# Recurrence levels as two masked 64-row blocks instead of four 32-row tiles, with single-buffered keys and another order of work

## The reference

```python
def wkv7_scan(r, decay, k, v, a, b, s0, reverse, return_y):
    '''S_t = S_{t-1} (diag(w_t) + a_t b_t^T) + v_t k_t^T ;  y_t = S_t r_t.  S: (B, H, N_value, N_key).'''
    xs = tuple(jnp.moveaxis(t, 1, 0) for t in (r, decay, k, v, a, b))

    def step(s, inp):
        rt, wt, kt, vt, at, bt = inp
        sa = jnp.einsum('bhvk,bhk->bhv', s, at)
        s = s * wt[:, :, None, :] + sa[..., None] * bt[:, :, None, :] + vt[..., None] * kt[:, :, None, :]
        y = jnp.einsum('bhvk,bhk->bhv', s, rt) if return_y else None
        return s, y
    ...
...
    for d, reverse in enumerate((False, True)):
        dc, kc, ac, bc = dirs_c[d]
        s_c, yc = wkv7_scan(r_c, dc, kc, vr_c, ac, bc, s0, reverse, with_ctx_out)
        dl, kl, al, bl = dirs_l[d]
        _, yl = wkv7_scan(r_l, dl, kl, vr_l, al, bl, s_c, reverse, True)
```

## Time and profile before

| | |
|---|---|
| median of 3 runs | 3984.77 us (3971.74 to 3986.89) |
| the profiled execution | 3977.56 us, its span 3975.8 us |
| PE busy | 3472.4 us, 87% of the span |
| PEld busy | 2580.4 us, 65% |
| DVE busy | 1563.2 us, 39% |
| ACT busy | 1099.8 us, 28% |
| POOL busy | 181.2 us, 5% |
| mean granted clock of TensorE | 0.928 of 2.4 GHz |
| opening of the recurrence | 395 to 423 us |
| the six steps | 423 to 852 us |

### The profile page before, as it was taken

How to read it: one execution, slowest core, us unless ns; L and a number is a source line. 1 busy time by engine, 2 the same in 40 slices (tenths; PEclk the granted TensorE clock), 3 DMA queues, 4 the chain that set the end, 5 groups by cost and what they waited for, 6 DMA issues and landing times. The chain is left out here.

```text
span 3975.8 us, 53364 instructions
## 1 busy us (share of the span) xinstructions
PE 3472.4 (87%) x23450; PEld 2580.4 (65%) x23450; DVE 1563.2 (39%) x2379; ACT 1099.8 (28%) x1728; POOL 181.2 (5%) x183
## 2 busy tenths in 40 slices
PE   6989778857888884999997799999999997799999
PEld 5854667744533332888785467887888785467877
DVE  3454655535211114333424544334333424543333
ACT  3235423211000002222323552223222323452222
POOL 0020221201000001000000000000000000000000
PEclk8989778868899996999998899999999999899999
DMA  6130000022599994222211022223222211022220
GB/s 226 64 124 0 3 3 3 3 84 85 212 419 421 421 421 155 85 90 101 85 43 69 1 75 85 95 96 97 93 85 103 88 43 69 1 74 85 85 106 38
DMA packets 173827, 441.02 MB, mean 111 GB/s; under 512 B 5794, under 2 KB 97692, under 8 KB 149020
## 3 DMA queue, kind: packets, MB, share of 16 engines
q1 hardware_dynamic: 173596, 437.61, 29.5%
HBM read 435.49 MB, written 2.10 MB: 110 GB/s over the span
## 5 line engine op out<-in xcount | busy, mean ns | idle before, releaser
L331 PE MATMUL banks<-mix_r,ring_r 128*128 128x512 f32 x1776 | 702.4, 396 | 0.0
L331 PE MATMUL banks<-mix_r,ffn_r 128*128 128x512 f32 x1664 | 666.6, 401 | 14.9 <-ACT mix_r L2324 7.8
L331 PE MATMUL banks<-h_r,ffn_r 128*128 128x512 f32 x1664 | 652.5, 392 | 0.0
L293 DVE TENSOR_TENSOR ring_r<-ring,ffn_r 128x2048 fp32r<-128x2048 f32 (+1 forms) x169 | 359.6, 2128 | 229.3 <-ACT ffn_r L290 226.5
L290 ACT ACTIVATE ffn_r<-ring 128x2048 fp32r<-128x2048 f32 (+1 forms) x169 | 301.3, 1783 | 479.1 <-PE banks L331 472.7
L331 PEld LDWEIGHTS banks<-mix_r,ring_r 128*128 128x128 f32 x1776 | 336.3, 189 | 83.6
L331 PEld LDWEIGHTS banks<-mix_r,ffn_r 128*128 128x128 f32 x1664 | 315.8, 190 | 84.2 <-issue 17.0
L331 PEld LDWEIGHTS banks<-h_r,ffn_r 128*128 128x128 f32 x1664 | 315.6, 190 | 73.6
L2501 PE MATMUL banks<-ring_r,ffn_r 128*128 128x512 f32 x704 | 279.2, 397 | 0.0
L2052 PE MATMUL banks<-ring,arena 128*64 128x512 f32 x1056 | 242.3, 613 | 37.1 <-DMA ring<-in_exp_w_down 23.3
L2500 PE MATMUL banks<-ffn_r 128*128 128x512 f32 x640 | 251.6, 393 | 4.7 <-DVE arena L2453 4.7
(11 more groups left out here) (419 smaller groups left out, 5220.6 us busy)
## 6 DMA issues: line engine op xcount, KB each, us to landing
ring<-in_exp_w_down SPq DMA_DIRECT2D x30, 2048.0 KB, 18.7
ring<-in_w_ffn_gate SPq DMA_DIRECT2D x44, 1024.0 KB, 5.3
ring<-in_w_ffn_up SPq DMA_DIRECT2D x44, 1024.0 KB, 7.9
ring<-in_w_ffn_down SPq DMA_DIRECT2D x20, 2048.0 KB, 7.7
ring<-in_exp_w_gate SPq DMA_DIRECT2D x18, 2048.0 KB, 17.6
ring<-in_exp_w_up SPq DMA_DIRECT2D x18, 2048.0 KB, 17.2
ring<-in_w_in SPq DMA_DIRECT2D x17, 2048.0 KB, 8.1
arena<-in_exp_w_gate SPq DMA_DIRECT2D x14, 2048.0 KB, 18.3
```

Source lines behind the costliest of these rows:

```text
L293: l.did(V.tensor_tensor(lo, x_, hi, ALU.subtract).then_inc(l.sem, 1), name, "lo", v)
L331: ins = TE.matmul(m[1](bank), m[2], m[3], start=m[4], stop=m[5])
```

## The change

The four 32x32 diagonal blocks of A become two 64x64 ones (`Am64`), whose masks (`levm`, now 64 columns) leave only the entries of a level; these lie within the 32x32 diagonal blocks, so X stays packed in 32 columns. A product of a level is then 16 matmuls for each direction, with 64 rows and 64 weight columns and 32 columns moved. The weights of `level_x`, `P1D`, are written by ACT twice from the same PSUM, once times a column of ones in the even 32-row blocks and zeros in the odd, once the other way round (`even`, `odd`, new columns of `hsel`), which puts a block in its place of the diagonal. `begin` makes X's start from the two halves of the masked product. `Al` has room for two levels instead of four, so POOL waits for `P1_made` of two levels before.

The keys have one buffer (`BK(d, e)`). `turn(0)` moves up between levels 2 and 3, `turn(1)` behind `whole_x`; `in_pe` for the next step comes after level 4 and after `turn(1)`, `cum_pe` after `pair_x` and after W. The grams run one to two places earlier, and `gram(1)` uses banks 2 and 3, own products banks 2, 3, 6, 7, U banks 6, 7 and Y banks 0, 1. In the opening both directions' `in_pe` and `cum_pe` come first, direction 1 in banks 0 and 1. The lists of ACT and DVE follow.

```diff
-    lev = np.zeros((2, P, 5, 32), np.float32)
-    c = s % 32
-    k = np.arange(32)[None, :]
+    lev = np.zeros((2, P, 5, 64), np.float32)
+    c = s % 64
...
-    hsel = np.kron(np.eye(2), np.ones((64, 1))).astype(np.float32)
+    hsel = np.concatenate([np.kron(np.eye(2), np.ones((64, 1))), (t[:, None] // 32) % 2 == np.arange(2)[None, :]], -1).astype(np.float32)
...
-                Am32, P1s, X64a = (hole.take(512) for _ in range(3))
-                sum_ = region(hole.at - 3 * 512, 2, 4, P)
-                spare1, spare2, spare3 = (hole.take(4, P) for _ in range(3))
+                sum_ = region(hole.at, 2, 4, P)
+                Am64, P1D = hole.take(16, 64), hole.take(16, 64)
+                P1s = P1D.rearrange("p g n -> p (g n)")[:, 0:512]
+                X64a = hole.take(512)
...
-                BK_even = high.take(2, 2, 4, P)
+                BK_ = high.take(2, 2, 4, P)
...
-                Al = high.take(4, 16, 32)
+                Al = high.take(2, 16, 64)
...
+                in_bank = lambda n, d: 0 if n == 0 and d == 1 else 2
+                even, odd = hsel[:, 2:3], hsel[:, 3:4]
...
                     l.wait_ge(*smalls["rwkv"])
                     in_pe(l, 0, 0)
+                    in_pe(l, 0, 1)
...
+                    cum_pe(l, 0, 0)
+                    cum_pe(l, 0, 1)
...
+                    w_dve(l, 0, 1)
...
-                        if j == 0:
-                            plus_dve(l, 0, 0)
-                    for t in range(NTA):
+                    plus_dve(l, 0, 0)
+                    plus_dve(l, 0, 1)
+                    for t in range(3):
                         vtm_copy(t)
                     kd_dve(l, 0, 0)
-                    l.wait_ge(*past(ro, "bonus_made"))
-                    l.did(V.tensor_copy(bonus.rearrange("p t c -> p (t c)"), banks[:, 4, 0:32]).then_inc(l.sem, 1), ro, "bonus")
+                    kd_dve(l, 0, 1)
+                    for t in range(3, NTA):
...
-                gram_bank = lambda q: 6 if q == 0 else 0
+                gram_bank = lambda q: 2 if q == 1 else 0
+                own_bank = lambda d: 6 if d else 2
...
                             elif q == 1:
                                 l.wait_ge(*past(co, "Amf", 0, 1))
-                            else:
+                            elif q == 2:
+                                l.wait_ge(*past(co, "Gm", 0, 1))
+                            elif q:
...
                             for g in range(8 * d, 8 * d + 8):
-                                for b in range(4):
-                                    ins = TE.matmul(cols_of(lower(d), g)[quad(b)], Al[quad(b), i - 1, g, :], XTp[quad(b), g, :],
-                                                    start=True, stop=True, tile_position=(32 * b, 32 * b))
+                                for hs in halves64:
+                                    ins = TE.matmul(cols_of(lower(d), g)[hs], Al[hs, i % 2, g, :], XTp[hs, g, :],
+                                                    start=True, stop=True, tile_position=(hs.start, hs.start))
...
                             l.wait_ge(*past(co, "P1", i, d))
                             if i == 1:
-                                l.wait_ge(*past(co, "Gm", 0, 1))
+                                l.wait_ge(*past(co, "Amf", 1, 1))
                             for g in range(8 * d, 8 * d + 8):
-                                for b in range(4):
-                                    ins = TE.matmul(cols_of(upper(d), g)[quad(b)], packed(P1s, d)[quad(b), g % 8, :], Xp[quad(b), g, :],
-                                                    start=True, stop=True, tile_position=(32 * b, 32 * b))
+                                for hs in halves64:
+                                    ins = TE.matmul(cols_of(upper(d), g)[hs], P1D[hs, g, :], Xp[hs, g, :],
+                                                    start=True, stop=True, tile_position=(hs.start, hs.start))
...
+                        gram(2)
+                        level_p(2, 0)
+                        level_p(2, 1)
+                        level_x(2, 0)
+                        level_x(2, 1)
+                        gram(3)
+                        turn(0)
+                        level_p(3, 0)
+                        level_p(3, 1)
+                        level_x(3, 0)
+                        level_x(3, 1)
+                        gram(4)
+                        level_p(4, 0)
+                        level_p(4, 1)
+                        level_x(4, 0)
+                        level_x(4, 1)
                         if more:
-                            l.wait_ge(*past(co, "Amf", 1, 1))
+                            l.wait_ge(*past(co, "BKt", 0))
                             in_pe(l, n + 1, 0)
-                        for i in (2, 3, 4):
-                            level_p(i, 0)
-                            level_p(i, 1)
-                            level_x(i, 0)
-                            level_x(i, 1)
-                            if i < 4:
-                                gram(i)
+                        gram(5)
+                        pair_p(0)
+                        pair_p(1)
+                        gram(6)
+                        pair_x(0)
+                        pair_x(1)
                         if more:
                             cum_pe(l, n + 1, 0)
-                        pair_p(0)
-                        pair_p(1)
-                        gram(4)
-                        pair_x(0)
-                        pair_x(1)
-                        gram(5)
                         whole_p()
+                        gram(7)
+                        whole_x()
+                        turn(1)
                         if more:
                             l.wait_ge(*past(nx, "Em", 0))
                             in_pe(l, n + 1, 1)
...
+                            cum_pe(l, n + 1, 1)
                         for d in range(2):
-                            l.wait_ge(*past(co, "XTf", d))
+                            l.wait_ge(*past(co, "XTf", 0))
+                            l.wait_ge(*past(co, "XTf", 1))
...
-                            for b in (0, 1):
-                                l.did(S.activation(packed(Am32, d)[quad(b)].rearrange("p (h j) n -> p h j n", h=2),
-                                                   banks[quad(b), 2 * d:2 * d + 2, :].rearrange("p h (j n) -> p h j n", j=4)[:, :, :, quad(b)],
-                                                   ACT.Copy).then_inc(l.sem, 1), co, "Am32", d)
+                            l.did(S.activation(Am64[0:64, 8 * d:8 * d + 8, :].rearrange("p (h j) n -> p h j n", h=2), own64(d, halves64[0]),
+                                               ACT.Copy).then_inc(l.sem, 1), co, "Am64", d)
...
-                            l.did(S.activation(packed(P1s, d), of32(lower(d)), ACT.Copy).then_inc(l.sem, 1), co, "P1", i, d)
+                            if i < 5:
+                                for x, part in enumerate((even, odd)):
+                                    l.did(S.activation(P1D[:, 8 * d:8 * d + 8, 32 * x:32 * x + 32], of32(lower(d)), ACT.Copy, scale=part)
+                                          .then_inc(l.sem, 1), co, "P1", i, d)
+                            else:
+                                l.did(S.activation(packed(P1s, d), of32(lower(d)), ACT.Copy).then_inc(l.sem, 1), co, "P1", i, d)
...
+                        keys(0)
+                        p1(4, 0)
+                        p1(4, 1)
...
+                        if more:
+                            exps_act(l, n + 1, 1)
...
-                            l.did(V.tensor_tensor(packed_x(d), packed(Am32, d), lm(d, 0), ALU.mult).then_inc(l.sem, 1))
+                            l.did(V.tensor_tensor(P1D[:, gs, :], Am64[:, gs, :], lm(d, 0), ALU.mult).then_inc(l.sem, 1))
+                            l.wait_ge(*l.own())
+                            l.did(V.tensor_tensor(packed_x(d), P1D[:, gs, 0:32], P1D[:, gs, 32:64], ALU.add).then_inc(l.sem, 1), co, "halves", d)
...
                         gm(0, 1)
+                        gm(1, 0)
                         add(1, 0)
+                        gm(1, 1)
                         add(1, 1)
                         gm(2, 0)
                         gm(2, 1)
+                        add(2, 0)
+                        add(2, 1)
                         gm(3, 0)
                         gm(3, 1)
+                        add(3, 0)
+                        add(3, 1)
+                        gm(4, 0)
+                        gm(4, 1)
                         add(4, 0)
                         add(4, 1)
                         if more:
+                            w_dve(l, n + 1, 0)
                         gm(5, 0)
                         gm(5, 1)
                         if more:
+                            kd_dve(l, n + 1, 0)
                         gm(6, 0)
                         gm(6, 1)
                         if more:
+                            plus_dve(l, n + 1, 0)
+                        pairs(0)
```

(53 more changed lines are left out.)

166 lines of the change are left out of this document (68 added, 98 removed).

## The result

The changed kernel takes 3993.2 us (median of 10 runs, 3988.3 to 4000.1), the kernel before 3977.3 beside it (10 runs, 3967.3 to 3990.2): a ratio of 1.0042, with a 95% interval of 1.0030 to 1.0054. So it is slower by some 16 us, 0.4%, where 3942 was forecast; the range, 3912 to 3975, misses it. The profiled execution took 3991.1 us (span 3989.3, before 3975.8).

A forecast was written before the change was run, and what follows sets the result against it. PE's level stage was taken as paced by instruction delivery, one 256-instruction block in 3.75 us. Savings of 5 x 6.2 + 8.0 + 0 = 39 us gave 3938.6 from the profiled 3977.6; with the runs' median, 3942, range 3912 to 3975.

The forecast's parts named there:

- The bound of the kernel before: Level stage: PE stops every 256 instructions, waiting for a block each 3.75 us; 51.0 us of idle time in the recurrence.
- The level products: PE's new 64-row units in the level stage: 0.96 us pitch against about 0.6, using the upper bound of 1.15 us.
- (c): Rival, slower: loads at 1.2 GHz make units 1.8 us through the level stage; 7.4 slower a step, 4022 us; chance 0.09.
- lower bound of 0.45: Level products: half the instructions in half the time, 0.45 us for one direction's 32 matmuls and loads.
- The chain of the level stage: Step 2 from level_p(1,0) at 562.7 to pair_p at 589.0: 26.3 us, pair_p 6.4 us earlier than before.
- I count one low bout as before: +2.3: Level stage: PE's clock is at 1.2 GHz for one 5 us bout, then returns; adds 2.3 us a step.
- The head: DVE's start of each step, ahead of the level products: 0.45 us more for each direction.
- doubling: Bound for the head: new add and larger multiply on DVE take twice as long beside POOL, 1.1 x 2 us.
- The tail: From pair_p to U, with work moved in and out: 0.2 us more a step, the last one 3.0 less.
- opening: Reordered work before the recurrence: pack at 425.6 instead of 426.0, taken as 0, bounds -2 and +3 us.
- (a): Rival, more: the level stage's low-clock bout vanishes because PE no longer stops; saves 53 us, 3925; chance 0.20.
- (b): Rival, nothing: each instruction block in the level stage still brings its stop; 0.6 us a step slower, 3981; chance 0.14.

The follow-up runs named there:

- e2: The changed kernel with each level product again as four 32-row tiles of 32 weight columns; 3997.3 us, ratio 1.0047 to the kernel before.
- e9: e6 with the four 32-row tiles of e2 in each level product; 3992.4 us, ratio 1.0050 to the kernel before.
- e5: The kernel before with 3 and 1 unused dense 128x512 products ahead of level_p(1,0) and level_p(1,1); 3974.5 us, ratio 1.0009.
- e10: The kernel before with 4 and 3 unused dense 128x512 products ahead of level_p(1,0) and level_p(1,1); 3987.9 us, ratio 1.0038.
- e6: The changed kernel with POOL's level-2 Al delayed and 4 and 3 unused dense products ahead of level_p(1,0) and level_p(1,1); 3935.8 us, ratio 0.9908.
- e4: The changed kernel with 3 and 1 unused dense 128x512 products ahead of level_p(1,0) and level_p(1,1); 3966.2 us, ratio 0.9971 to the kernel before.
- e8: The changed kernel with one unused dense product ahead of each of levels 2, 3 and 4, none in the head; 3985.5 us, ratio 1.0031.
- e3: The changed kernel with POOL's Al of level 2 waiting for the second transpose of level 0; 3981.7 us, ratio 1.0010 to the kernel before.
- e1: The kernel before with only the changed kernel's new opening; 3975.1 us, ratio 0.9991.

## Why the prediction was wrong, step by step

**The bound of the kernel before was read rightly.** The stops were the delivery of instructions: they vanish with half the instructions (after), return with twice as many (e2, e9), and hardly care for the clock (e5, e10). In the recurrence of before no two packets of the instruction queue are less than 3.3 us apart. The instruction queue of the changed kernel has 5 packets in 555 to 590 us, where the earlier trace rows have 8 in 30.

**The level products: right.** A unit has a pitch of 1.03 us (forecast 0.96) at 2.4 GHz and 1.8 at 1.2, as the upper bound and rival (c) said. The lower bound of 0.45 is out. The columns moved don't set the time: whole_p, with twice as many behind loads of the same form, had 1.15 for its 32 at 2.4 GHz, `level_p` has 1.12. The load's columns fit; its rows doubled as well, and no run separates the two.

**The chain of the level stage: right at the clock it assumed.** e6 has 26.3 us, the number of the forecast. They agree a bit by luck: the forecast's 26.3 holds 2.3 for a low bout, e6's 2.8 for three dense products. e4's step 0 is the cleaner measure of the chain: 24.6 at 1.00, against 24.0 without the bout, and level_p(1,1) 3.2 us behind level_p(1,0) as the forecast's 3.3 asked.

**The step that failed: "I count one low bout as before: +2.3".** That is some 5 us at 1.2 GHz a stage, 30 in all. From the clocks of the six stages after (0.75, 0.70, 0.66, 0.70, 0.51, 0.52) the low time is 2 x (1 - clock) of each, 162 us of 219.7. In it a unit takes 1.8 instead of 1.03, so I estimate 43% of it as lost, 70 us, where 14 were counted. The missing 56 and the 1.6 us by which level_p(1,1) came late (below), 10 over six steps, make the 63 or so by which the level stages missed the forecast. The kernel before was low too, for 122 us by the same sum (clocks 0.69, 0.67, 0.74, 0.71, 0.67, 0.68 in its six stages; two of them, cut by hand, in the earlier trace rows), but a microsecond at 1.2 GHz costs the changed kernel more: its unit goes from 1.03 to 1.8 us, one of 32-row tiles from 0.65 to some 0.9 (e2), and it has no waits for instructions left in which slower units could hide. How much of the low clock such waits covered before was not separated; e5's 10 us for 27 us less of it say that it did pay. e4 and e6 show the cause: with the same products at 1.00 the stages are 24.6 to 26.4.

The argument for it was a single window: "after 5.00 busy of 5 at 0.50 the next stretch had 0.99". In the new stream PE is as busy, and stays low with 5.00 busy of 5 for 15 us (step 2), 30 (step 4) and 35 (step 5). The Trainium skill (TensorE: Matmul & The Clock Gate, Why this matters for your kernels) advises to keep TensorE continuously busy in order to get past the low clock; the traces here do not bear out busy time as the remedy: with 64x32 products and their loads, busy 5.00 of 5 did not do it. With its warning of gaps they agree in part: all six falls of the changed kernel come during, or up to 2.1 us behind, pauses of 2.6 to 3.8 us ahead of the products of level 1. But three of e4's four follow pauses of only 1.64 or 1.65, and its step 4 has the same pause and no fall. With 128x512 products ahead of them the clock held (e6), and with such products between them it came back in part (e8). What in the small products fails to count, columns moved or the share that loads take, was not separated; nor why it returned near gram and turn(0) in steps 0 to 3 of the changed kernel and not in 4 and 5.

**The head: mis-sized.** I gave 0.42 us to the add of halves and 0.83 to plus-one. This is DVE in the head of direction 1 of step 2, then POOL:

```profile
555.03 0.69 DVE L1621 TENSOR_TENSOR arena<-arena,ring 128x512 f32<-128x512 f32 x1
555.76 1.38 DVE L1623 TENSOR_TENSOR arena<-arena 128x256 f32<-128x256 f32 x1
557.17 1.37 DVE L1625 TENSOR_TENSOR arena<-arena 128x256 f32<-128x256 f32 x1
558.58 0.45 DVE L1614 STREAM_TRANSPOSE arena<-arena 128x256 f32<-128x256 f32 x1
```

```profile
555.07 5.83 POOL L1728 TENSOR_TENSOR arena<-arena,ring 128x512 f32<-128x512 f32 x4 [2.16 <-DVE arena L1602]
```

Beside POOL's multiply the add takes 1.37 us, and so does plus-one, of the same shape, which takes 0.42 where POOL is idle. The transpose ends at 559.03 and level_p(1,1) starts at 559.12: the page names POOL as its releaser, but POOL's Al(1,1) is the first of the four that the row joins, a quarter of 5.83 us; it was DVE. The forecast had doubling as its bound, and it was tripling, because POOL's operation had itself grown from 0.81 us to 1.44 (forecast 1.3): a DVE instruction with two operands in SBUF seems to wait for the end of POOL's one, so that the length of the latter sets the price. Instruction by instruction, POOL's first two multiplies of that row end at 556.85 and 558.26, and the add and plus-one 0.28 us behind each. The Trainium skill (SBUF — State Buffer, SBUF: two separate sides) calls the port that the two share an exclusive lock; e3, where L1625, no longer beside POOL, is at 0.43 again, agrees. In all the heads grew by 5.8 instead of 2.4 us, and level_p(1,1) comes 4.9 us after level_p(1,0) instead of 3.3 (6.0 in step 5). PE's waits ahead of the products of level 1, where the clock falls, grew with it, from 13.3 to 29.6 us.

**The tail and the opening.** The tails fell by 6.6 us, forecast 2.0: right in sign and small. The opening is zero (28.0 against 27.6; e1). Keys in one buffer made nothing late: no wait of PE on them stands in the recurrence.

**The rivals.** (c), slower by the loads at 1.2 GHz, came true in its mechanism. It asked for a stage 13.6 us above 26.3 if low throughout, 39.9 (its terms add up to 40.9, so 14.6 above); steps 4 and 5 have 42.2. It was to decide "from about half the stage at 1.2 GHz beyond the bout counted"; 162 of 219.7 us are 74%, 60% without the 30 counted. It got a chance of 0.09, because I took the forecast's own slower units, which leave PE no idle time, for its cure. (a) asked for the low bout to go away without the stops; that took dense products (e6). (b) is out: no stop is left in the bursts, and e2's sum of stages shows by chance the same time.

## What to carry to other kernels

Before you take away a bound, price the stage at the low clock that the trace already shows in it, with the units that it will have then: a wait may be hiding part of it. A dense burst of small products need not bring the clock back. Fill the pause ahead of it with a few wide ones, and judge both changes together, since either alone showed little here. When POOL's operation grows, a DVE operation with two SBUF operands beside it can grow as well, as the 128x256 adds did here.

## What was not expected of the hardware

- PE at 5.00 busy of 5 stayed at 0.50 for 30 us (after, step 4) and 35 us (step 5), when nearly all it had were 64x32 products with their loads and a few grams.
- After 10 us at 1.00 with 5.00 busy of 5, one pause of 1.65 us ahead of small products was followed by 30 us at 0.50 (e4, step 1); the same pause in its step 4 was followed by a stage wholly at 1.00.
- A 128x256 add on DVE took 0.42 us alone, 0.83 beside POOL's multiply of 0.81, and 1.37 beside those of the changed kernel, 1.44 on average.
